# Every second low part of the modulated features moves from GpSimd to VectorE

## The reference, cut to what matters

```
h_x = modulate(rms_norm(x, norm_g[l, 0]), sh1_x, sc1_x)     # h * (1 + scale) + shift
h_c = modulate(rms_norm(ctx, norm_g[l, 0]), sh1_c, sc1_c)
f_x = squared_relu_mlp(modulate(rms_norm(x, norm_g[l, 2]), sh2_x, sc2_x), w_mlp_in[l], w_mlp_out[l])
```

## Time and profile before

| | us |
|---|---|
| median of 3 runs | 1590.78 |
| lowest and highest of them | 1589.05, 1591.47 |
| the profiled execution | 1591.33 |
| its span, first to last instruction | 1589.4 |
| mean granted TensorE clock in it | 0.983 |

### The profile page before, as it was taken

The page is one execution under the profiler, slowest core; times in us unless marked ns, Lnnn a source line. Parts: engine busy times, 40 slices in busy tenths (PEclk is TensorE's granted clock), DMA queues, the critical chain, the costliest instruction groups (busy, mean ns, idle before and its releaser), DMA issues.

```text
span 1589.4 us, 24201 instructions
## 1 busy us (share of the span) xinstructions
PE 1524.4 (96%) x9562; PEld 1304.0 (82%) x9562; DVE 859.9 (54%) x1472; ACT 677.3 (43%) x1096; POOL 172.6 (11%) x165
## 2 busy tenths in 40 slices
PE   9999899999999989999799999999998999889998
PEld 7998698999996865786689777777787887779997
DVE  5786655554545864347465443433447546655444
ACT  5454344545445334426454222231225446544443
POOL 3100220000000110000414001110002020021110
PEclk9999999999999989999899999999999999989999
DMA  6456565453436315211213443544512421235451
GB/s 253 176 188 228 214 223 182 162 199 134 164 128 239 136 63 203 107 53 54 80 59 127 160 185 133 212 163 155 212 54 90 142 75 54 92 147 203 168 199 67
DMA packets 43769, 233.81 MB, mean 147 GB/s; under 512 B 13264, under 2 KB 14224, under 8 KB 16784
## 3 DMA queue, kind: packets, MB, share of 16 engines
q1 hardware_dynamic: 31232, 222.38, 37.5%
q10 hardware_dynamic: 12432, 9.94, 2.1%
HBM read 231.22 MB, written 1.08 MB: 146 GB/s over the span
## 4 chain that ended last, share of the span: by engine, by line
PE 45%; DVE 3%; POOL 1%; ACT 1%; issue 1%; DVEq 0%; ACTq 0%
PE ps L552 13%; PE ps L554 13%; PE ps L553 13%; PE ps L764 2%; PE ps L650 1%; DVE wlo L1044 1%; PE ps L702 1%; PE ps L736 1%; POOL flo L2281 1%; ACT whi L1034 0%; PE ps L612 0%; PE ps L634 0%; POOL mix L2319 0%; ACT fhi L1093 0%; DVE mix L1969 0%
## 5 line engine op out<-in xcount | busy, mean ns | idle before, releaser
L1044 DVE TENSOR_TENSOR wlo<-raw,whi 128x2048 fp32r<-128x2048 f32 x162 | 381.5, 2380 | 250.6 <-ACT whi L1034 250.3
L552 PE MATMUL ps<-fhi,whi 128*128 128x256 f32 (+1 forms) x1280 | 391.2, 306 | 9.4 <-DVE wlo L1044 3.9
L1034 ACT ACTIVATE whi<-raw 128x2048 fp32r<-128x2048 f32 x162 | 304.5, 1906 | 211.8 <-PE ps L554 162.9
L554 PE MATMUL ps<-fhi,wlo 128*128 128x256 f32 (+1 forms) x1280 | 387.3, 303 | 0.0
L553 PE MATMUL ps<-flo,whi 128*128 128x256 f32 (+1 forms) x1280 | 387.2, 302 | 0.0
L552 PEld LDWEIGHTS ps<-fhi,whi 128*128 128x128 f32 x1280 | 245.9, 192 | 33.0 <-issue 9.5
L553 PEld LDWEIGHTS ps<-flo,whi 128*128 128x128 f32 x1280 | 246.0, 192 | 8.8
L554 PEld LDWEIGHTS ps<-fhi,wlo 128*128 128x128 f32 x1280 | 245.8, 192 | 8.9
L552 PE MATMUL ps<-whi,fhi 128*128 128x512 f32 (+1 forms) x592 | 209.1, 353 | 9.7 <-DVE e_b L2116 4.5
L553 PE MATMUL ps<-wlo,fhi 128*128 128x512 f32 (+1 forms) x592 | 205.3, 347 | 0.0
L554 PE MATMUL ps<-whi,flo 128*128 128x512 f32 (+1 forms) x592 | 205.2, 347 | 0.0
(11 more groups left out here) (249 smaller groups left out, 1805.0 us busy)
## 6 DMA issues: line engine op xcount, KB each, us to landing
raw<-in_wstream SPq DMA_DIRECT2D x210, 1024.0 KB, 5.0
gates<-gated ACTq DMA_DIRECT2D x6, 512.0 KB, 4.0
hx<-in_x SPq DMA_DIRECT2D x1, 1024.0 KB, 5.2
lnrow<-in_ln_g ACTq DMA_DIRECT2D x2, 512.0 KB, 3.9
lnrow<-in_ln_b ACTq DMA_DIRECT2D x2, 512.0 KB, 5.9
hc<-in_ctx ACTq DMA_DIRECT2D x1, 1024.0 KB, 7.4
mix<-in_rpb_rows ACTq DMA_DIRECT2D x4, 256.0 KB, 3.6
hc<-in_rpb_rows ACTq DMA_DIRECT2D x4, 256.0 KB, 3.7
```

The costliest lines, as they stand in the source:

```text
L552: mm(o, lh, rh, start=start, stop=False)
L554: return mm(o, ll, rh, start=False, stop=stop)
L1034: nc.scalar.activation(whi[:, w % SPLIT_SLOTS, :], raw[:, c % RAW_SLOTS, :], ACT.Copy).then_inc(*did("scalar", ("hi", w)))
L1044: nc.vector.tensor_tensor(wlo[:, w % SPLIT_SLOTS, :], raw[:, c % RAW_SLOTS, :], whi[:, w % SPLIT_SLOTS, :].bitcast(F32), ALU.subtract).the ...
```

## The change

VectorE gets low parts 1 and 3 of each call: `modulate` has an inner `low(j)` that waits for high part j and subtracts, and calls `low(1)` behind modulation 2 and `low(3)` behind modulation 3. GpSimd's `low_modulated` loops over j = 0 and 2 alone. Readers wait for low parts 1 and 3 on VectorE's semaphore instead of GpSimd's; the waits of the other instructions are as they were.

```diff
--- before.py
+++ after.py
@@ -1598,6 +1598,15 @@
 
             def modulate(name, l, which, g, before=None, A=None, B=None):
 
+
+                def low(j):
+
+                    cols = slice(g * S, g * S + S)
+                    dve.wait_ge(*after("fhi", name, j))
+                    v.tensor_tensor(flo[:, 2 * j:2 * j + 2, cols], ftmp(l, which, g, j).rearrange("p (a b) -> p a b", a=2),
+                                    fhi[:, 2 * j:2 * j + 2, cols].bitcast(F32), ALU.subtract).then_inc(
+                        *did("vector", ("split", name, j)))
+
                 for j in range(4):
                     dve.wait_ge(*after(name, j))
                     if j >= 2 or before:
@@ -1610,6 +1619,8 @@
                         ins = v.tensor_scalar(ftmp(l, which, g, j)[:, q * S:(q + 1) * S], src(name, j)[:, q * S:(q + 1) * S],
                                               factor, shift, ALU.mult, ALU.add)
                     ins.then_inc(*did("vector", ("modulated", name, j), ("read", name, j)))
+                    if j >= 2:
+                        low(2 * j - 3)
 
             def rsqrt(out_, in_, n, e):
 
@@ -2275,7 +2286,7 @@
             p = nc.gpsimd
             def low_modulated(name, l, which, g):
 
-                for j in range(4):
+                for j in (0, 2):
                     pool.wait_ge(*after("fhi", name, j))
                     cols = slice(g * S, g * S + S)
                     p.tensor_tensor(flo[:, 2 * j:2 * j + 2, cols], ftmp(l, which, g, j).rearrange("p (a b) -> p a b", a=2),
```

## The result

The changed kernel takes 1598.86 us (median of 4 executions, 1596.59 to 1600.14) where the kernel before takes 1590.03 (median of 4, 1589.05 to 1591.47). The ratio is 1.0053, with a 95% interval of 1.0036 to 1.0071, so the change costs 5.7 to 11.3 us. The forecast was 1601.1 in a range of 1594 to 1606. The profiled execution took 1596.59 (span 1594.8), the lowest of the four. All executions in this document are fast ones but one of low part 3 alone (2140.04 us at a mean granted clock of 0.651), which its ratio leaves out.

What follows compares the result with a forecast made beforehand. The prediction took TensorE as the bound (busy 1524.4 of 1589.4 us), so only its waits count. Call delays of 8.6 us, with 1.7 for the clock 10.3, gave 1601.6, or 1601.1 as median; range 1594 to 1606.

Steps and rivals of the forecast that it cites:

- The order within a call: In each modulate call: modulation 2 unmoved, modulation 3 0.5 us later, VectorE idle about 0.7 before low part 3.
- The three queue calls: ("n1",0,1), ("n1",0,0), ("n1",1,0): TensorE waits for work behind the call in VectorE's queue; +2.0 us each.
- ("n1",1,1) and ("n2",1,0): Calls at 1221.1 and 1396.3: TensorE's release follows high part 3 or modulation 3; +0.5 us each.
- ("n2",0,1) and ("n2",0,0): Calls at 819.3 and 842.6: VectorE instructions held back by GpSimd get shorter; -0.1 and 0 us.
- "f1": Call at 185.0: GpSimd's `gain_shift` starts earlier and blocks VectorE's low part 3; TensorE +1.7 us, bounds -0.1 to +2.0.
- The clock: TensorE's gap at 539 becomes 2.45 us, and its granted clock falls behind it: +1.7 us.
- the clock at 561: TensorE's gap there was 2.68 us already; a longer one may stretch the slow part, 0 to 1 us.
- The cover at 1220: The clock falls behind the 2.7 us gap at 1207, but 1.52 us of TensorE waiting until 1220.43 absorbs it: 0.
- Rival 3: VectorE's queue delay is covered, TensorE waiting for something else: only +1 to +3 us, 1592 to 1594; chance 0.13.
- Rival 4: The last low part decides in every call: 0.1 us gained each, at most 0.8, 1590.0 us; chance 0.07.
- rival 2: The clock falls in "f1" as well and stays down longer at 561: +13 us, 1604; chance 0.2.
- Rival 1: The same delays in the calls without a fall of the clock: +8.6 us, 1599.4; chance 0.2.

Runs made afterwards that it cites:

- low part 3 alone: Kernel before, with VectorE making only low part 3 behind modulation 3 in all eight calls, GpSimd the other three: ratio 1.0016.
- repetition: The whole change run again beside the kernel before, also called "the whole change, again": 1597.98 us, ratio 1.0054.
- the queue calls alone: Kernel before, with the change only in ("n1",0,1), ("n1",0,0) and ("n1",1,0): 1596.32 us, ratio 1.0043.
- low part 1 alone: Kernel before, with VectorE making only low part 1 behind modulation 2 in all eight calls, GpSimd the other three: ratio 1.0015.

## Why the prediction was right, and where it wasn't

- *The order within a call.* Right: M2 unmoved, M3 0.5 later, the idle 0.70 before low part 3 in all eight calls, no subtraction at 1.3 (15 of 16 at 0.68 to 0.69). Undoing one subtraction at a time gave 0.46 and 1.40 of the gap at 561.
- *The three queue calls, +2.0 each.* Right in place, 8% too large: 1.81, 1.85, 1.85. I added up durations, and a following instruction starts 0.07 sooner. Alone they make the ratio 1.0043, where the whole change makes it 1.0054.
- *("n1",1,1) and ("n2",1,0), +0.5 each.* The gaps went from 4.54 to 5.00 and from 3.55 to 3.88: 0.46 and 0.33. At ("n2",1,0) the reading that M3 alone releases TensorE doesn't quite hold: TensorE started 0.53 after M3's end before and 0.36 after it now. What else it waited for is open.
- *("n2",0,1) and ("n2",0,0), -0.1 and 0.* The two instructions that GpSimd had held back took 0.16 and 0.42 for 0.63 and 1.35, as predicted, and TensorE's 0.21 at 826 was gone:

```profile
827.88 0.16 DVE L2006 TENSOR_TENSOR sumh<-sumh 128x2 f32<-128x2 f32 x1
...
851.03 0.42 DVE L2035 TENSOR_TENSOR htmp<-htmp 128x256 f32<-128x256 f32 x1
```

- *"f1", +1.7.* 1.63 in the profile, by the mechanism named: low part 3 was expected to end at 194.05, and ended at 194.35 in a call that began 0.33 later. The experiments put the overlap at 1.3 to 1.85. The Trainium skill's page "SBUF — State Buffer", section "Who interferes with whom", has the rule that a VectorE instruction with two SBUF inputs contends with a GpSimd instruction that reads SBUF, and that the order of issue decides which one is blocked. The row of 2.53 us and, in the other order, the one of 2.91 us agree with it.
- *The clock, +1.7 for a fall at 539.* This term failed. "New gaps are 0.44 + 2.0 = 2.45 at 539, where I expect the fall": the gap became 2.25 in the kernel after and 2.23 in its repetition, and in the 5 us behind it the granted clock stayed at 1.00. The forecast had named "a gap of 2.4 without the clock falling" as a sign of being wrong; it came at 2.25, the same length that was its example of a fall. It did fall in the kernel with the queue calls alone, where the gap was 2.48, and there the stretch from 514 to 561 took 51.04 instead of 49.65. The windows behind the gap, of the kernel after and of that one (busy of the engines, PEclk, DMA share, GB/s):

```profile
542.00:547.00 5.00, 4.73 (x21) 3.96 (x22) 4.79 (x10) 0.03 (x1) 0.00 (x0) 1.00 0.73 270
```

```profile
539.00:544.00 5.00, 4.36 (x12) 3.48 (x13) 4.79 (x9) 0.16 (x1) 0.00 (x0) 0.66 0.62 229
```

What I counted too low is the clock at 561. With a gap there of 3.14 to 4.53 the stretch to 587 took 26.9 to 27.2 in seven kernels of eight, where the kernel before had 25.94 with the same gaps: 1.0 to 1.3 us more, which I had as "0 to 1". The exception is the profiled execution of the kernel after (25.85). So a clock term of 1.0 to 1.3 us is there, at another place than forecast. The executions' mean clocks say the same of the whole: span times (1 - clock) averages 29.5 us over the six of the whole change, again, and 27.4 over the 17 of the kernel before beside it, so an estimated 2.2 us more (standard error 0.9) went to the lower clock, part of it perhaps in waits, where it costs nothing. That this is near the forecast's 1.7 is luck, since the fall that the 1.7 stood for did not happen.

- *The cover at 1220.* Right: at 1210.94 the clock was down (the first matmul took 0.79, and 0.50 before), and the loss went into the 1.52 that the transposes had waited.

The sum without the clock was 8.6 us; by the calls it measured 1.63 + 1.81 + 1.85 + 1.85 + 0.46 + 0.33 - 0.1 = 7.8, or 7.5 with 1.3 for "f1". The medians say 8.8 and 8.3. That the rest is the clock, at 561 among other places, fits the stretches and the mean clocks, but the intervals (5.7 to 11.3 and 6.4 to 10.8 us) are too wide to show it. Rival 3 (a covered queue) is out by the gaps: the one marked "issue" at 539 was 0.44 before and 1.07, 1.20, 2.01 and 2.25 with low part 1, low part 2, low part 3 and low parts 1 and 3 on VectorE. Rival 4 (the last low part decides) is out, since the gaps grew where it had none to grow, and rival 2 (1604) is above the highest execution (1600.14, and 1600.70 in the repetition). Rival 1 (the same delays, no fall, 1599.4) is nearer to the measured 1598.86 than the forecast, and it describes the gap at 539 rightly. One slip in the chances: rival 3's 1592 to 1594 lies within 3.2 us of 1590.8, so its 0.13 belonged to "no change", which makes that 0.17 and not 0.1.

## What to carry to other kernels

Moving work from an idle engine to a less idle one is priced by what stands behind it in the new engine's queue, and by the wait that it brings along: here low part 3 was 0.6 us of subtraction and 0.8 us of waiting for another engine's result, and three chains behind it felt both. Look for the place where the new engine idles already, and before dividing work anew look at what makes it idle: in this kernel one more buffer was worth more than any division that was tried. With an engine freed early, ask what it starts next, and beside whom.

## What the runs showed that was not expected

- Behind a TensorE gap of 2.2 to 3.5 us the clock fell in some executions and not in others, so in these runs the length of the gap alone doesn't tell. It fell behind 2.25 at 93 in the earlier trace rows and behind 2.48 at 539, and stayed at 1.00 behind 2.25 at 542. At 789, where no code is changed, the gap is 3.47 in the profile of the kernel after and 3.49 in the repetition; the 7 us from 789 ran at 1.00 in the one and 0.53 in the other. This is most likely why their stretches 787-1233 differ by 2.8 us with the same gaps. At 561 a gap of 2.68 was followed by a stretch of 25.94, one of 2.34 by 25.99, one of 2.69 by 24.48 and one of 1.44 by 24.48, with the same gaps of 4.0 in each. The 6 us from 561 ran at 0.72 for the 25.94 and at 1.00 for the 24.48 behind 2.69.
- One kernel's executions can lie on two levels 6 us apart, with their mean granted clocks apart as well (low part 1 alone, nothing from 1591.4 to 1594.8). For effects below 5 us the gaps of a profile told more than the medians.
